# A second gate buffer per side in the expert loop of a hybrid encoder step, with the residual rows kept in memory meanwhile

## The reference, cut to what matters

```python
def _grouped_moe(h, router_w, router_bias, w_gate, w_up, w_down):
    scores = jax.nn.sigmoid(h @ router_w)             # 16 experts in 4 groups
    # the best group, and in it the 2 best experts, for each token
    # assignments are sorted by expert; each expert's rows are padded to whole blocks
    def expert_block(args):
        xb, e = args
        return (jax.nn.silu(xb @ w_gate[e]) * (xb @ w_up[e])) @ w_down[e]
    # y[token] = sum over its 2 experts of weight * expert_block row

x = x + g_f * f.reshape(bsz, L, D_MODEL)              # residual
return _rmsnorm(x, norm_final_w)
```

## Times and profile before

| | us |
|---|---|
| median of 3 runs | 2685.18 |
| lowest, highest | 2683.52, 2692.44 |
| the profiled execution | 2692.73 |
| its span | 2690.9 |
| mixers and output projection, to about | 1985 |
| expert loop, TensorE | 2075.4 to 2633.0 |
| last stage | 2633 to the end |

### The profile page before, as it was taken

How to read it: one execution, slowest core, us unless ns; L and a number is a source line. 1 busy time by engine, 2 the same in 40 slices (tenths; PEclk the granted TensorE clock), 3 DMA queues, 4 the chain that set the end, 5 groups by cost and what they waited for, 6 DMA issues and landing times.

```text
span 2690.9 us, 39173 instructions
## 1 busy us (share of the span) xinstructions
PE 2516.2 (94%) x16348; PEld 1562.4 (58%) x16348; DVE 1006.0 (37%) x1780; ACT 709.2 (26%) x1252; POOL 66.9 (2%) x66
## 2 busy tenths in 40 slices
PE   6998999999999999999999999999997899989994
PEld 3555888885555566655555556765455444434443
DVE  4356455453223045552342548722345001101115
ACT  3132222221111111120243046731024222222224
POOL 0000000000000000000000000000000000000003
PEclk9999999999999999999999999999998999999997
DMA  7000212204000111141003011131306656657436
GB/s 313 32 32 32 75 47 106 75 31 158 32 32 31 36 52 61 58 162 71 32 18 150 32 38 40 37 118 67 109 21 268 222 209 267 238 229 286 168 135 221
DMA packets 65269, 291.99 MB, mean 109 GB/s; under 512 B 8956, under 2 KB 32068, under 8 KB 44612
## 3 DMA queue, kind: packets, MB, share of 16 engines
q1 hardware_dynamic: 52996, 255.92, 25.2%
q0 software_dynamic: 8928, 22.03, 2.4%
q10 hardware_dynamic: 3168, 11.54, 1.1%
HBM read 694.20 MB, written 56.63 MB: 279 GB/s over the span
## 4 chain that ended last, share of the span: by engine, by line
PE 79%; DMA 8%; DVE 6%; ACT 5%; issue 2%; SPq 1%; POOL 0%; DVEq 0%; ACTq 0%; POOLq 0%
PE psum L531 30%; PE psum L675 15%; PE psum L1519 8%; DMA arena<-in_moe 7%; PE psum L1377 4%; PE psum L1503 4%; PE psum L1102 3%; PE psum L630 2%; ACT arena L1758 2%; PE psum L560 1%; PE psum L1090 1%; PE psum L1015 1%; PE psum L991 1%; PE psum L1488 1%; PE psum L1082 1%
## 5 line engine op out<-in xcount | busy, mean ns | idle before, releaser
L531 PE MATMUL psum<-arena 128*128 128x384 f32 x2544 | 826.8, 487 | 10.9 <-DVEq L330 6.1
L531 PEld LDWEIGHTS psum<-arena 128*128 128x128 f32 x2544 | 483.0, 190 | 352.9 <-issue 10.5
L675 PE MATMUL psum<-arena 128*128 128x384 f32 (+1 forms) x1920 | 541.0, 427 | 6.4 <-ACT arena L689 3.3
L675 PEld LDWEIGHTS psum<-arena 128*128 128x128 f32 x1920 | 341.6, 193 | 155.1 <-issue 6.8
L1519 PE MATMUL psum<-arena 128*32 128x256 f32 x5632 | 325.7, 387 | 31.6 <-DMA arena<-in_moe 30.4
L1519 PEld LDWEIGHTS psum<-arena 128*32 128x32 f32 x5632 | 178.5, 112 | 164.8 <-DMA arena<-in_moe 37.6
L1503 PE MATMUL psum<-arena 128*32 128x512 f32 x1408 | 160.8, 594 | 10.1 <-DMA arena<-in_moe 9.5
L1927 ACT ACTIVATE arena<-psum 32x512 f32<-32x512 f32 x176 | 103.6, 589 | 226.6 <-PE psum L1503 225.0
L1377 PE MATMUL psum<-arena 128*128 128x512 f32 (+1 forms) x384 | 126.0, 487 | 0.3 <-issue 0.3
L2614 DVE TENSOR_TENSOR arena<-arena,psum 128x256 f32<-128x256 f32 x44 | 18.5, 421 | 278.0 <-PE psum L1519 188.1
L689 ACT ACTIVATE arena<-psum 128x384 f32<-128x384 f32 x96 | 46.7, 490 | 277.0 <-PE psum L675 216.7
(11 more groups left out here) (539 smaller groups left out, 2409.6 us busy)
## 6 DMA issues: line engine op xcount, KB each, us to landing
arena<-in_moe SPq DMA_DIRECT2D x532, 1024.0 KB
arena<-in_ada SPq DMA_DIRECT2D x12, 2048.0 KB, 8.8
gate_raw<-arena SPq DMA_DIRECT2D x96, 192.0 KB, 1.8
arena<-gate_raw SPq DMA_DIRECT2D x8, 2304.0 KB, 8.3
y_rows<-arena ACTq DMA_DIRECT2D x22, 512.0 KB
arena<-in_gate SPq DMA_DIRECT2D x5, 2048.0 KB, 8.4
arena<-in_br SPq DMA_DIRECT2D x4, 2048.0 KB, 8.1
arena<-in_qkv SPq DMA_DIRECT2D x3, 2048.0 KB, 15.1
```

Source lines behind the costliest of these rows:

```text
L531: last = nc.tensor.matmul(pset(s)[:, n, :], w[:, kk, :], src[:, kk, n * N3:(n + 1) * N3], start=(kk == 0), stop=(kk == K - 1))
L675: last = nc.tensor.matmul(bank(6 + u % 2)[:, cols * p:cols * (p + 1)], w[:, m % 4, kk, :], HT[:, kk, n * N3 + cols * p:n * N3 + cols * (p ...
```

## The change

The gate weights get a second buffer per side. `gset[i][0]` is the old place, for even steps, `gset[i][1]` is new, for odd steps; the two new ones lie at `R0` and `R0 + 4096`, on the rows of `X`. So `X` is stored to DRAM (`x_kept`) chunk by chunk when it has been turned, and read back (`x_back`) after the last gate product. SP issues the gate load for step j+2 in iteration j (`gates_ahead`), as one DMA of 2.1 MB per side instead of two halves, conditional on the expert of step j+2 differing from that of step j, for which VectorE makes a second table (`eint2`). Up and down weights keep their single buffers. TensorE waits once per step for the whole gate instead of twice.

```diff
+        gset = [[cut(0, 4096), cut(R0, 4096)], [cut(WSET, 4096), cut(R0 + 4096, 4096)]]
+        x_back = [cut(R0 + D * s, D) for s in range(NT)]
+        x_kept = nc.dram_tensor("x_kept", (T, D), F32, kind="Internal").ap()
...
             sp.dma_start(gate_rows, gate_t).then_inc(m_grow, 16)
+            def keep_rows(c0, c1):
+                for c in range(c0, c1):
+                    sp.wait_ge(m_htok, 2 * NT + 1 + 2 * (c + 1))
+                    sp.dma_start(x_kept[c * P:(c + 1) * P].rearrange("p (k f) -> p k f", k=KD),
+                                 X[:, :, c * P:(c + 1) * P]).then_inc(s_pstate, 16)
+            keep_rows(0, 3)
             sp.wait_ge(m_route, ROUTE_E0)
...
+            sp.dma_start(gset[1][0], first[1][:, 0:4096]).then_inc(e_wg[0], 16)
+            for q in range(2):
+                a = 4096 + 2048 * q
+                sp.dma_start(wset[1][:, a:a + 2048], first[1][:, a:a + 2048]).then_inc(e_wu[q], 16)
+            keep_rows(3, 6)
...
             sp.dma_start(gate_p, grow[0:1].to_broadcast([P, D])).then_inc(m_grow, 16)
+            keep_rows(6, NT)
             sp.wait_ge(m_route, ROUTE_TAB)
+            sp.wait_ge(s_pstate, STATES + 16 * NT)
+            for i in range(2):
+                sp.dma_start(gset[i][1], part_expert(1, i)[:, 0:4096]).then_inc(e_wg[1], 16)
+            def gates_ahead(j):
+                sp.wait_ge(e_g, 2 * (j - 1))
+                for i in range(2):
+                    at = NST * i + j
+                    e, differs = part_expert(j, i), sp.value_load(eint2[:, at:at + 1], min_val=0, max_val=1)
+                    sp.dma_start(gset[i][j % 2], e[:, 0:4096], cond=(differs > 0)).then_inc(e_wg[j % 2], 16)
...
-                    for at, used, done in ((0, e_g, e_wg), (4096, e_u, e_wu)):
-                        for q in range(2):
-                            sp.wait_ge(used, 2 * j + q + 1)
-                            for i in range(2):
-                                a = at + 2048 * q
-                                sp.dma_start(wset[i][:, a:a + 2048], then[0][i][:, a:a + 2048], cond=(then[1][i] > 0)).then_inc(done[q], 16)
-                if 1 <= j < NST:
+                    for q in range(2):
+                        sp.wait_ge(e_u, 2 * j + q + 1)
+                        for i in range(2):
+                            a = 4096 + 2048 * q
+                            sp.dma_start(wset[i][:, a:a + 2048], then[0][i][:, a:a + 2048], cond=(then[1][i] > 0)).then_inc(e_wu[q], 16)
+                if 1 <= j:
...
+                if j + 2 < NST:
+                    gates_ahead(j + 2)
                 now = then
+            sp.wait_ge(e_g, 2 * NST)
+            for s, c in enumerate(CHUNKS):
+                sp.dma_start(x_back[s], x_kept[c * P:(c + 1) * P]).then_inc(e_wg[0 if s < 4 else 1], 16)
...
-                        pe.wait_ge(ready[q], 32 * (j + 1) + 16)
+                        if w:
+                            pe.wait_ge(e_wu[q], 32 * (j + 1) + 16)
+                        elif q == 0:
+                            pe.wait_ge(e_wg[j % 2], 32 * (j // 2 + 1) + (0 if j % 2 else 16))
...
+            V.then(tt(erow2[:, 2:NB], erow[:, 0, 2:NB], erow[:, 0, 0:NB - 2], ALU.not_equal))
+            V.then(nc.vector.tensor_copy(eint2[:, 2:NB], erow2[:, 2:NB]))
...
-                    xc = X[:, :, c * P:(c + 1) * P]
+                    xc = hd(x_back[s], KD)
```

More of the change, by code:

```diff
@@ L460, in build @@
         wset = [cut(0, 12288), cut(WSET, 12288)]
+        gset = [[cut(0, 4096), cut(R0, 4096)], [cut(WSET, 4096), cut(R0 + 4096, 4096)]]
+        x_back = [cut(R0 + D * s, D) for s in range(NT)]
+        x_kept = nc.dram_tensor("x_kept", (T, D), F32, kind="Internal").ap()
+        erow2, eint2 = s5p[0:1, 0:NB], s5p[0:1, 128:128 + NB].bitcast(INT)
+        GATES_EVEN, GATES_ODD, STATES = 16 + 32 * (NST // 2), 32 * (NST // 2), 64
         xg = [cut(12288, D), cut(13312, D)]
@@ L882, in _ @@
                     sp.wait_ge(o_fill, 3 * KD)
-                    for at, done in ((0, e_wg), (4096, e_wu)):
-                        for q in range(2):
-                            a = at + 2048 * q
-                            sp.dma_start(wset[0][:, a:a + 2048], A["moe"][0][:, a:a + 2048]).then_inc(done[q], 16)
+                    sp.dma_start(gset[0][0], A["moe"][0][:, 0:4096]).then_inc(e_wg[0], 16)
+                    for q in range(2):
+                        a = 4096 + 2048 * q
+                        sp.dma_start(wset[0][:, a:a + 2048], A["moe"][0][:, a:a + 2048]).then_inc(e_wu[q], 16)
             sp.wait_ge(m_htok, 2 * NT + 1)
             sp.dma_start(gate_rows, gate_t).then_inc(m_grow, 16)
+            def keep_rows(c0, c1):
[4 more added lines that the diff above has]
+            keep_rows(0, 3)
             sp.wait_ge(m_route, ROUTE_E0)
@@ L897, in _ @@
             e0 = sp.value_load(eint[:, 0, 0:1], min_val=0, max_val=NE - 1)
[L898 to L906, removed]
+            sp.dma_start(gset[1][0], first[1][:, 0:4096]).then_inc(e_wg[0], 16)
[3 more added lines that the diff above has]
+            keep_rows(3, 6)
+            sp.wait_ge(e_wg[0], 32)
+            sp.dma_start(gset[0][0], first[0][:, 0:4096], cond=(e0 > 0)).then_inc(e_wg[0], 16)
+            for q in range(2):
+                a = 4096 + 2048 * q
+                sp.wait_ge(e_wu[q], 32)
+                sp.dma_start(wset[0][:, a:a + 2048], first[0][:, a:a + 2048], cond=(e0 > 0)).then_inc(e_wu[q], 16)
             sp.wait_ge(m_ht, 2 * NT)
@@ L917, in _ @@
             sp.dma_start(gate_p, grow[0:1].to_broadcast([P, D])).then_inc(m_grow, 16)
+            keep_rows(6, NT)
             sp.wait_ge(m_route, ROUTE_TAB)
+            sp.wait_ge(s_pstate, STATES + 16 * NT)
[7 more added lines that the diff above has]
+                    sp.dma_start(gset[i][j % 2], e[:, 0:4096], cond=(differs > 0)).then_inc(e_wg[j % 2], 16)
             now = None
-            for j in range(NST + 1):
+            for j in range(NST):
                 then = None
@@ L1511, in _ @@
                 x = xT[j // 2 % 2]
-                for w, ready, s in ((0, e_wg, e_g), (1, e_wu, e_u)):
+                for w, s in ((0, e_g), (1, e_u)):
                     for q in range(2):
-                        pe.wait_ge(ready[q], 32 * (j + 1) + 16)
+                        if w:
+                            pe.wait_ge(e_wu[q], 32 * (j + 1) + 16)
+                        elif q == 0:
+                            pe.wait_ge(e_wg[j % 2], 32 * (j // 2 + 1) + (0 if j % 2 else 16))
                         for k in range(4 * q, 4 * q + 4):
@@ L1518, in _ @@
                                     o, a = 64 * i + 32 * h, P * k + 64 * i + 32 * (j % 2)
+                                    gw = wset[i][:, 4096:8192] if w else gset[i][j % 2]
                                     last = nc.tensor.matmul(bank(w)[o:o + 32, 0:256], x[:, a:a + 32],
-                                                            wset[i][:, 4096 * w + 512 * k + 256 * h:4096 * w + 512 * k + 256 * (h + 1)],
+                                                            gw[:, 512 * k + 256 * h:512 * k + 256 * (h + 1)],
                                                             start=(k == 0), stop=(k == KD - 1))
@@ L2624, in _ @@
                     y0, y1 = yg[s]
-                    xc = X[:, :, c * P:(c + 1) * P]
+                    xc = hd(x_back[s], KD)
+                    if s in (0, 4):
+                        dve.wait_ge(*((e_wg[0], GATES_EVEN + 16 * 4) if s == 0 else (e_wg[1], GATES_ODD + 16 * (NT - 4))))
                     dve.wait_ge(f_y[s % 4], 32 * (s // 4 + 1) + (16 * (NGB // 2) if s % 4 >= 2 else 0))
```

## The result

The changed kernel takes 2734.39 us (median of 4 runs, 2729.67 to 2737.08) against 2687.45 us for the kernel before in the same comparison: a ratio of 1.0172, 95% interval 1.0147 to 1.0196; the medians lie 46.9 us apart. Its profiled execution took 2737.08 us, with a span of 2735.3 us; that of before had 2690.9 us.

| stretch (us) | before | after | difference | forecast |
|---|---|---|---|---|
| span's start to step 0 | 2075.40 | 2075.07 | -0.3 | 0 |
| step 0 to step 2 | 29.65 | 45.54 | +15.9 | +21 |
| step 2 to step 43 | 512.87 | 536.70 | +23.8 | +36 |
| step 43 to the end | 72.98 | 77.99 | +5.0 | +3 |

The account below looks back on a forecast made before the run. TensorE carried 79% of the chain; its 39.9 us of weight waits were all the change could win. Start 21, loop 26, clock 10 and end 3 made +60 us: 2752.7 profiled, 2745 as a median, range 2710 to 2778.

Parts of the forecast that it names:

- rival (a): The forecast itself: start, loop and end all lose time, 2745 us, chance 0.68.
- Part 1: Gate loads in SP's queue: still start 3.3 us into the step before use, leaving 7.5 or 8.7 us.
- Rival (c): Loop: gate loads run ahead and waits before gate and up products go; -10 us, 2675, chance 0.09.
- the gates are issued before T(J-1): Sign against the forecast: gates for step J issued before step J-1 starts; no size given.
- Part 2: Expert loop, steps 2 to 42: gate bytes double at expert changes; +26 us, ends +5 and +40.
- The middle steps: Steps 15, 20, 28, wanting 4.2 MB of gates at once: 4 to 6 us of wait.
- Part 3: TensorE's clock after long idles: some six more idles of 3 us and more, +10 us, ends +3 and +18.
- Part 4: Start, before step 1: X's stores, the wait for them and 4.2 MB of gates; +21 us, ends +14 and +25.
- the round trip: Start: SP waits for all nine X stores, reads two registers, then waits for the first byte; +5.2 us.
- Part 5: The rest: X's loads back delay the last stage, +3 us, ends 0 and +6; VectorE's operations at most 0.5.
- rival (e): SP's queue becomes the bound through register reads and issues: +20 to +40 us more, 2775, chance 0.07.
- rival (b): Only start and end lose time, loop waits stay about as long: 2712 us, chance 0.13.

Follow-up runs that it names:

- e1: Changed kernel with gate loads issued behind the up loads, ahead of the down waits, and six register reads per iteration instead of eight: 2719.27 us, ratio 1.0123.
- e5: Changed kernel with the second gate load of each expert change left out (stale weights, wrong output): 2710.86 us, ratio 1.0084.
- e3: Changed kernel without the stores of X, the wait for them and the loads back (wrong output): 2718.76 us, ratio 1.0107.
- e9: Kernel before plus the nine stores and nine loads of X, single gate buffers, no wait for the stores before the loop: 2700.60 us, ratio 1.0053.
- e6: e1 with the second gate load of each expert change left out (wrong output): 2690.55 us, ratio 1.0007.
- e7: Kernel before, single buffers, the gate loaded once more in the step after each change, two more register reads per iteration: 2723.93 us, ratio 1.0135.

## Why the prediction was right

The forecast was +60 us and a time of 2745; it came out at +47 and 2734, inside the range, and its rival (a) was the one that happened. The doubled loads and the spill are the cause, as forecast. The total lies 13 us under the forecast, because the start and the waits of the loop came out 5 and 11 us below their terms, and the end 2 above. By its own steps:

**Part 1, no real lead.** Right in kind: in most steps SP issues the gates inside the step before their use. The place was off for one side: I put all four register reads in front of both loads, but `gates_ahead` reads two, issues, reads two, issues. Side 0 goes out at 1.9 us instead of 3.3. Two of the signs that I had named came true without their meaning. Rival (c) was to show by a gate issued over 9 us before its step; side 0's goes out 10.2 us before step 8, and the kernel is slower all the same. And for steps 16, 21, 24 and 29 the gates are issued before T(J-1), which was to prove me wrong; the start of the load alone did not decide. In the table, the second buffer in this order only repays the whole gate's 11.4 us (524.3 to 513.0), and e1 shows 14.8 us more for the mended place. That these 11.4 us are lost and won back was in none of my terms; that they cancel is luck of the sum.

**Part 2, twice the bytes.** The mechanism is shown by e5 against the change, the same program with only those loads gone: 23.7 us (536.7 to 513.0), waits and clock together. The term was mis-sized. The idles grew by 15.0 us outside step 1 (68.1 - 20.0 + 1.9, less 30.4 - 4.9 + 9.5), where I had +26. By group: 14 to 16 +5.5, 19 to 21 +4.7, 27 to 29 +7.0, together 17.2 for 21 forecast; steps 23 and 24 -1.2 for +5; the isolated changes -1.0 for 0. The middle steps were as worked out (5.54, 4.37, 6.12 us, forecast 4 to 6), and from side 0's issue to use their 4.2 MB took 16.2 us at step 15 and 15.1 at step 20 (forecast 12.4 to 13.7, and up to 2.5 more). The 7.5 us for 2.1 MB with nothing between follows from none of the rows given; the single gates that ended a wait at steps 27, 31 and 4 took 8.7 to 9.1 us from issue to use. Steps 21 and 29 waited 2.70 us each, and step 16 did not wait at all, where I had 1 to 4. At 23 and 24 the kernel before lost 12.7 us in gates, ups and downs, the changed one loses 11.5: of the ups only the last half still waits (2.02 us) and the downs hardly do (0.56 us), more than I had granted it.

**Part 3, the clock.** +10 forecast. The stretch grew by 23.8 and its idles by 15.0; the remaining 8.8 us are matmuls at the lower clock, which the group's busy time repeats (334.9 - 325.7 = 9.2). The granted clock in step 15 was 0.72:

```profile
2286.00:2297.00 11.00, 10.37 (x133) 6.06 (x134) 0.39 (x1) 0.38 (x1) 0.00 (x0) 0.72 1.02 427
```

The size was right, the rule behind it less so: I had let only idles of 3 us and more cost clock, but of two idles of 2.70 us the one before step 21 cost nothing (7.11 us for 128 matmuls) and the one before step 29 cost 1.7 us (8.80).

**Part 4, the start.** 7.4 us for 4.2 MB instead of 1.05 MB fits the 7.3 that remain in e3, within the 2 us by which this stretch varies. The spill was mis-sized: 9 for bytes and 5.2 for the round trip, and it came to 8.8 (e9: 7.2 without the wait for all stores, 1.6 with it). The table of stretches of the changed kernel shows the round trip (a row ends with PEclk, DMA share and GB/s):

```profile
2086.00:2092.00 6.00, 0.00 (x0) 0.00 (x0) 0.43 (x1) 0.00 (x0) 0.00 (x0) 0.62 1.00 318
2092.00:2094.00 2.00, 0.00 (x0) 0.00 (x0) 0.00 (x0) 0.00 (x0) 0.00 (x0) 0.50 0.05 14
2094.00:2096.00 2.00, 0.00 (x0) 0.00 (x0) 0.00 (x0) 0.00 (x0) 0.00 (x0) 0.50 0.66 156
```

The queue stands nearly empty for about 3 us, not 5, and SP issues the gates at 2093.85 (first L938), where I had it at about 2098. Part of that is the time to the first byte, which I had put at 2 us: the first packet of the gates moved about 1 us after the issue, and the same holds at step 23 of the kernel before, where after an issue at 2355.76 the engines moved 90, 180 and 352 GB/s in the three microseconds from 2356 on. I had counted that slow beginning as waiting. Another part is the stores: from 2088 to 2091 they moved at some 347 GB/s, so 1.5 us each and not 1.75. How many of the middle three fell into the slack around 2070, for which I had allowed 1.5 us in all, was not tried apart.

**Part 5, the end.** +3 forecast with an end of 6, +5.0 measured, and the row that I had named, scatter to first gather, holds it. SP did not become the bound (rival e): steps without loads still take 10.85 us (2171.38 to 2182.23 is step 6); rival (b) is excluded by the loop's +23.8, rival (c) by its sign.

What stays open: why the same 15 loads cost 23.7 us in the change, 32.8 between e6 and e1 and 34.9 in e7. In e7 the later gate loads may be part of it; for the other two no run shows the reason.

No run beats the kernel before. e6 shows what would have to be had: two buffers in the mended order with each expert's gate loaded once, 23.7 us less in the loop, against some 21 us for the start and the end. That needs a buffer chosen by the number of changes so far, so an address in TensorE's products that is known only at run time. It was not tried.

## What to carry to other kernels

A second buffer used by even and odd steps doubles the traffic wherever a weight stays for several steps: count the bytes of every load, not only the time at which the buffer comes free. Then write down where in the issuing queue's program the new load stands and what it waits behind; a buffer that is free two steps ahead is worth only what that queue's order lets through. Splitting a load in two, so that the first part is issued as soon as its place is free and used as soon as it is there, was worth more here (11.4 us) than one larger transfer.

## What the runs showed of the hardware

- Issuing a store of X with 512-byte runs can hold SP itself. The line's instructions in the changed kernel, ns min, median, max; and time to landing:

```profile
L899 SPq DMA_DIRECT2D x_kept<-arena x9: 513/592/9663, 2045.3 to 2085.0; - x9
...
DMA to landing us min/median/max: 3.6/11.3/17.4
```

  Four of the nine issues took 3.5 to 9.7 us, all of them with loads and stores queued in front (the DMA engines' busy share was 0.92 to 1.16); the issue of a gate load that moves data took 0.34 us (L938). I had not expected this. In the changed kernel SP had to wait for these stores anyway; in e9 it had not, and its first gate load for step 1 stood behind 14.6 us of such issues.
- An idle of 20.02 us in front of step 1 cost TensorE no more afterwards (9.71 us for 128 matmuls) than one of 4.88 us before (9.95). Two idles of 2.70 us cost differently: 7.11 us for 128 matmuls at a granted clock of 1.00 behind the one (step 21, 2369 to 2377), 8.80 at 0.81 behind the other (step 29, 2490 to 2499).
